# The first product of two squared-relu layers by seven half-size products

## Chip, core and metric

The kernel runs on one core of one Trainium2 chip. The metric is the device time of one execution in microseconds. The core has TensorE (PE, matrix products), VectorE (DVE), ScalarE (ACT), GpSimd (POOL) and SyncE (SP, which here issues the transfers).

## What is computed

Three transformer layers over 512 tokens of width 1024, all in float32. The first has two SwiGLU parts and a mixer, the second and third a mixer each and then a squared-relu part. The change touches the two squared-relu parts:

```python
def sq_relu_mlp(h, w1, w2):
    u = jax.nn.relu(h @ w1)
    return (u * u) @ w2
...
        x = x + sq_relu_mlp(rmsnorm_2(x, norm_mlp[layer]), w_mlp1[layer], w_mlp2[layer])
```

Here `w1` is 1024 x 4096 and `w2` is 4096 x 1024.

## The kernel before

**Layout.** Activations are held transposed, features on the 128 partitions and the 512 tokens along the row. A tile is 128 features by 512 tokens; the width 1024 is 8 tiles, the inner width 4096 is 32.

**Three matmuls for one.** To keep float32 accuracy each operand is split into a rounded part and a remainder: `hi` by an ACT copy to fp32r and `lo = x - hi` by a DVE subtract. Each product is then hi.hi + hi.lo + lo.hi, three matmuls into the same PSUM bank. Weights stream from memory in the order of `stream_plan()`, as chunks of 128 x 1024 (8 blocks of 128 x 128) that SP loads into two raw buffers `wraw`; ACT makes `whi` (L2130) and DVE `wlo` (L2435), in four buffers each (`NW = 4`). The step "split" c stands in the queues of SP, ACT and DVE. It may run when chunk c - 4 has been used by PE (`used[c - 4]`).

**The order.** `work_order()` writes out one list of steps; each engine walks this list in order and does its own part of each step, with semaphore waits between engines. `opened(key)` puts the splits of up to three chunks ahead, and `split_free` puts one when its buffer's chunk is closed, so a split stands in the queues ahead of the work on an earlier tile's result.

**A squared-relu part, `mlp(l, s, end, nxt)`.** It runs in two halves. For each of 16 feature tiles PE does 24 matmuls of 512 columns with `hhi`/`hlo` (the normalised input's parts); then the step "relu" makes the inner activation: DVE takes max(0) times the per-token scale `rb` from PSUM (L2541), ACT squares (L2173) and copies to `mhi` (L2176), DVE subtracts to get `mlo` (L2544). DVE's queue stands still between its two instructions until ACT is done:

```python
                    dve.scalar_tensor_tensor(tmps[:, q, :], banks[b][:, :], 0.0, rb[:, :], MAX,
                                             MUL).then_inc(*relu.up((s, f)))
                    w.wait_ge(*v_hi[s, f])
```

After 16 tiles come 8 output tiles of 48 matmuls each (two chunks), added to the stream `ya` by "resid" (L2536). The first four feature tiles of a part are special: three are done side by side (`side_by_side`), between them the sums of squares for the norm are paid and the reciprocal root is worked out on DVE ("rstd"), then the fourth tile runs, PE spreads the scale (L1946), ACT copies it to `rb` (L2147), and the four "relu" steps follow.

POOL does nothing in these parts before the change. Its instructions in the other stages are adds and multiplies of 128 x 512. In the mixing stage it works beside DVE: L2919 and L2925 are rotary products and sums.

## Time and profile before

| | us |
|---|---|
| median of 3 runs (2445.96 to 2446.32) | 2446.11 |
| the profiled execution, first to last instruction (its span) | 2446.3 |
| TensorE busy | 2390.1 |
| VectorE busy | 1234.3 |
| ScalarE busy | 962.0 |
| GpSimd busy | 196.0 |

The profiled execution's span stands for its own time; it lies 0.2 us above the median of the runs. "Busy" is the time in which at least one instruction of the engine was in work. Matmuls overlap in the trace, so that the pace of PE is read from the distance between starts, not from the duration of one. The first squared-relu part lies at 1482 to 1860 us, the second at about 2075 to 2440 us.

### The profile page before, as it was taken

Reading aid. Unit: us, or ns where it says so; the run is one execution under the profiler, and the core shown is the slowest. Engines: PE = TensorE matmul, PEld = TensorE weight load, DVE = VectorE, ACT = ScalarE, POOL = GpSimd, SP = SyncE. Lnnn points to the kernel's source line nnn. Section 1 sums busy time; section 2 is a strip of 40 time slices with the busy share of each in tenths; the row PEclk is TensorE's granted clock in tenths of the full one; section 3 lists DMA queues with packets and bytes.
Section 4 is the critical chain, followed back from the end, with each engine's and each line's share of the span. In section 5 each row is a group of like instructions: output and inputs, shape, how many; then the busy total and the mean of one; then the engine's idle time right before and its main releaser. Section 6 shows DMA issues by size and latency. Waiting matters only on the chain.

```text
span 2446.3 us, 28445 instructions
## 1 busy us (share of the span) xinstructions
PE 2390.1 (98%) x11206; PEld 1912.1 (78%) x11206; DVE 1234.3 (50%) x2012; ACT 962.0 (39%) x1613; POOL 196.0 (8%) x147
## 2 busy tenths in 40 slices
PE   8999999999999999999999999999999899999998
PEld 7888888777777788888887677888887677888887
DVE  5533436788654445433336855424435775532432
ACT  4323224455432334322323554313324785431432
POOL 0100100322102000100100200000001100000000
PEclk9999999999999999999999999999999999999999
DMA  4323323211222232323323113322232012333332
GB/s 144 104 87 103 98 88 102 77 52 52 70 69 72 63 108 81 101 80 110 95 83 99 59 53 103 104 94 95 95 96 64 29 46 80 97 101 95 95 95 70
DMA packets 66805, 208.50 MB, mean 85 GB/s; under 512 B 7408, under 2 KB 15856, under 8 KB 66416
## 3 DMA queue, kind: packets, MB, share of 16 engines
q1 hardware_dynamic: 66672, 206.68, 27.1%
q8 instruction: 89, 1.46, 0.2%
q14 instruction: 44, 0.36, 0.0%
HBM read 204.55 MB, written 2.10 MB: 84 GB/s over the span
## 4 chain that ended last, share of the span: by engine, by line
PE 90%; DVE 4%; ACT 3%; issue 2%; DMA 1%; POOL 0%; POOLq 0%; SPq 0%; ACTq 0%; DVEq 0%
PE bank L1842 26%; PE bank L1846 26%; PE bank L1844 26%; PE bank L2009 2%; PE bank L1971 1%; PE bank L2016 1%; PE bank L2000 1%; PE bank L2062 1%; ACT whi L2130 1%; PE bank L1917 1%; DVE wlo L2435 1%; PE bank L1913 1%; PE bank L1915 1%; DMA wraw<-in_stream 1%; PE bank L1936 1%
## 5 line engine op out<-in xcount | busy, mean ns | idle before, releaser
L2435 DVE TENSOR_TENSOR wlo<-wraw,whi 128x1024 fp32r<-128x1024 f32 (+5 forms) x436 | 487.9, 1122 | 541.9 <-ACT whi L2130 541.1
L1842 PE MATMUL bank<-hhi,whi 128*128 128x512 f32 x1736 | 693.2, 399 | 11.4 <-ACT whi L2130 9.4
L1846 PE MATMUL bank<-hhi,wlo 128*128 128x512 f32 x1736 | 681.7, 393 | 2.1 <-DVE wlo L2435 2.1
L1844 PE MATMUL bank<-hlo,whi 128*128 128x512 f32 x1736 | 680.7, 392 | 0.4 <-DVE hlo L2442 0.4
L2130 ACT ACTIVATE whi<-wraw 128x1024 fp32r<-128x1024 f32 (+5 forms) x436 | 408.9, 940 | 493.2 <-PE bank L1846 425.0
L1842 PEld LDWEIGHTS bank<-hhi,whi 128*128 128x128 f32 x1736 | 328.1, 189 | 84.2 <-ACT whi L2130 11.4
L1846 PEld LDWEIGHTS bank<-hhi,wlo 128*128 128x128 f32 x1736 | 327.7, 189 | 74.9 <-DVE wlo L2435 5.1
L1844 PEld LDWEIGHTS bank<-hlo,whi 128*128 128x128 f32 x1736 | 328.2, 189 | 67.3 <-DVE hlo L2442 2.2
L1844 PE MATMUL bank<-mlo,whi 128*128 128x512 f32 x576 | 227.8, 395 | 0.2 <-DVE mlo L2742 0.2
L1842 PE MATMUL bank<-mhi,whi 128*128 128x512 f32 x576 | 227.8, 396 | 0.0
L1846 PE MATMUL bank<-mhi,wlo 128*128 128x512 f32 x576 | 227.7, 395 | 0.0
L1842 PEld LDWEIGHTS bank<-mhi,whi 128*128 128x128 f32 x576 | 108.1, 188 | 26.7 <-ACT mhi L2287 0.4
L1844 PEld LDWEIGHTS bank<-mlo,whi 128*128 128x128 f32 x576 | 108.1, 188 | 26.7 <-DVE mlo L2742 0.5
L1846 PEld LDWEIGHTS bank<-mhi,wlo 128*128 128x128 f32 x576 | 108.1, 188 | 26.3
L2173 ACT ACTIVATE tmps<-tmps 128x512 f32<-128x512 f32 x64 | 40.5, 632 | 175.1 <-DVE tmps L2541 175.1
L2906 POOL TENSOR_TENSOR tmps<-tmps 128x512 f32<-128x512 f32 x44 | 56.5, 1285 | 613.7 <-DVE tmps L2511 464.6
L2536 DVE TENSOR_TENSOR ya<-ya,bank 128x512 f32<-128x512 f32 x71 | 48.3, 685 | 111.5 <-PE bank L1846 111.5
L2273 ACT ACTIVATE tmps<-bank 128x512 f32<-128x512 f32 x88 | 52.6, 598 | 99.5 <-PE bank L2009 97.6
L2544 DVE TENSOR_TENSOR mlo<-tmps,mhi 128x512 fp32r<-128x512 f32 x64 | 44.4, 693 | 87.3 <-ACT mhi L2176 87.3
L2919 POOL TENSOR_TENSOR ftmps<-ftmps,rs 128x512 f32<-128x512 f32 x31 | 45.2, 1459 | 377.4 <-DVE ftmps L2611 377.2
L2541 DVE SCALAR_TENSOR_TENSOR tmps<-bank,rb 128x512 f32<-128x512 f32 x64 | 44.1, 690 | 59.9 <-PE bank L1846 55.4
L2511 DVE TENSOR_TENSOR tmps<-bank,rb 128x512 f32<-128x512 f32 x44 | 30.4, 690 | 85.7 <-PE bank L1846 85.7
(419 smaller groups left out, 3094.7 us busy)
## 6 DMA issues: line engine op xcount, KB each, us to landing
wraw<-in_stream SPq DMA_DIRECT2D x343, 512.0 KB, 3.5
wraw<-in_stream SPq DMA_DIRECT2D x32, 192.0 KB, 2.4
wraw<-in_stream SPq DMA_DIRECT2D x22, 256.0 KB, 2.6
wraw<-in_stream SPq DMA_DIRECT2D x26, 128.0 KB, 2.0
wraw<-in_stream SPq DMA_DIRECT2D x8, 320.0 KB, 2.9
xa<-in_x SPq DMA_DIRECT2D x8, 256.0 KB, 6.4
out<-ya SPq DMA_DIRECT2D x8, 256.0 KB, 2.7
m<-in_mask SPq DMA_DIRECT2D x1, 1024.0 KB, 4.8
```

The lines of the kernel that those rows point to most:

```text
L1842: pe.matmul(out, sh, xh, start=first, stop=False)
L1844: pe.matmul(out, sh, xl, start=False, stop=False)
L1846: p = pe.matmul(out, sl, xh, start=False, stop=end and last)
L2009: p = pe.transpose(banks[tb][:, i * 128:i * 128 + 128], src[:, at0:at0 + 128], ident[:, :])
L2130: act.activation(whi[j][:, 0:L], wraw[i][:, 0:L], F.Copy).then_inc(*hi.up(c))
L2273: act.activation(et_of(stage, et)[:, c * 128:(c + m) * 128], banks[tb][:, 0:m * 128], F.Copy).then_inc(*turned.up((stage, u, c)))
L2435: dve.tensor_tensor(wlo[j][:, 0:L], wraw[i][:, 0:L], whi[j][:, 0:L].bitcast(f32), SUB).then_inc(*lo.up(c))
L2536: dve.tensor_tensor(ya[:, n, :], ya[:, n, :], banks[b][:, :], ADD).then_inc(*x_dve.up((nxt, n)))
L2541: dve.scalar_tensor_tensor(tmps[:, q, :], banks[b][:, :], 0.0, rb[:, :], MAX, MUL).then_inc(*relu.up((s, f)))
L2544: dve.tensor_tensor(ahl[s][1][:, f % 16, :], tmps[:, q, :], ahl[s][0][:, f % 16, :].bitcast(f32), SUB).then_inc(*v_lo.up((s, f)))
L2906: pool.tensor_tensor(tmps[:, q, :], tmps[:, q, :], tmps[:, u, :], MUL).then_inc(*gated.up((s, f)))
L2919: pool.tensor_tensor(s, s, rs[rows, :], MUL).then_inc(*rope_sin.up(key))
```

## The change

**Products.** Of each part's 32 feature tiles the first four are done as before. The other 28 go in seven blocks of four tiles. A block is a 2 x 2 product: weights 512 inputs by 256 features, activations 512 inputs by 256 tokens. In place of eight such products, `seven(f)` does seven (`q1, q7, p5, p6, q2, q4, q3`), each 24 matmuls of 256 columns into one bank; three of them go on top of an earlier one's bank. A fifth to eighth operand are sums: four of the seven weight chunks are sums that POOL makes in place in the raw buffer (`plus`, with `settled` naming the chunk whose `lo` must be made first), and four token operands are differences or sums of quarters of the input, made once for each part.

**Token operands.** POOL writes the gained input into `xa` (eight "plain" of 128 x 512), then four "token_sum" of 128 x 1024; ACT and DVE split them into `thi`/`tlo` ("token_parts"). They stand in the list behind the three side-by-side tiles, "token_parts" behind the first four "relu".

**Combining.** "first_copy" (ACT) saves q1's bank, "shared" (DVE, two instructions) builds the two common terms V and W in `ftmps`, and four "corner" steps give the quarters of the result: DVE adds or subtracts (not for `c11`), takes max and scale, ACT squares and copies, DVE subtracts.

**Stages.** A part now runs in four quarters of 8 feature tiles (two blocks; in the first quarter the four plain tiles and one block), each followed by 8 output tiles of 24 matmuls; the inner buffer holds 8 tiles in place of 16. The first two output tiles do their first four inputs ahead (`begun`), then the rest. The part has four more raw buffers, six in all.

```diff
+PRODUCTS = (("q1", 0, None, None), ("q7", 0, 1, "q1"), ("p5", 1, 2, None), ("p6", 0, 2, "q7"), ("q2", 3, None, None),
+            ("q4", 2, None, None), ("q3", 0, 3, "p6"))
+NARROW, WIDE = 2, 6
...
+    def seven(tag, blk, s, quarters):
+        at = len(raws)
+        for pair in quarters:
+            raws.append(Raw(pair, s))
+        index = {}
+        for name, raw, plus, settled in PRODUCTS:
+            index[name] = len(plan)
+            plan.append(Chunk((tag, blk, name), at + raw, 8, 128, None if plus is None else at + plus,
+                              None if settled is None else index[settled]))
+        for raw, name in ((0, "q3"), (1, "p5"), (2, "q4"), (3, "q3")):
+            raws[at + raw].gone = index[name]
...
     def mlp(l):
-        for half in range(2):
-            for f in range(16):
-                col(f"m{l}u{half}", f"mlp1_{l}", half * 16 + f)
+        s, mat = 4 + 2 * l, f"mlp1_{l}"
+        for part in range(4):
+            for b in range(2):
+                f = 8 * part + 4 * b
+                if f == 0:
+                    for n in range(4):
+                        col(f"m{l}u", mat, n)
+                else:
+                    seven(f"m{l}s", f, s, rows_and_cols([mat] * 4, (f + 2, f + 3, f, f + 1)))
             for n in range(8):
-                col(f"m{l}d{half}", f"mlp2_{l}", n, 16, half * 16)
+                add((f"m{l}d{part}", n, 0), f"mlp2_{l}", part * 8, 8, n * 128, 128, s)
...
     def mlp(l, s, end, nxt):
-        afree = (end, *x_at[7])
+        guard = afree = (end, *x_at[7])
+        put("wide", s, guard)
...
+        def seven(f):
...
+            bank, last = {}, {}
+            over = {"q2": "q1", "q4": "q7", "q3": "p5"}
+            for name, *_ in PRODUCTS:
+                c = opened((f"m{l}s", f, name))
+                if name in over:
+                    b, was = bank[over[name]], (last[over[name]],)
+                else:
+                    b = G.take()
+                    was = b.was
+                bank[name] = b
+                put("seven", s, name, c, b.i, was, name not in over)
+                closed.add(c)
+                done = ("used", c)
+                key = (s, f)
+                if name == "q1":
+                    put("first_copy", key, b.i, V.i, (done, *V.free))
+                    last["q1"] = ("first_copy", key)
+                elif name == "p6":
+                    put("shared", key, b.i, bank["q7"].i, V.i, W.i, (done, *W.free))
+                    b.free = (("combined", ("v", key)),)
+                    last["q7"] = ("combined", ("w", key))
+                    q = T.take()
+                    put("corner", key, "c22", bank["p5"].i, W.i, q.i, ("combined", ("w", key)), q.was, afree)
+                    last["p5"] = W.free = ("combined", (key, "c22"))
+                    W.free = (W.free,)
+                    q.free = (("v_lo", (key, "c22")),)
+                elif name in over:
+                    part = {"q2": "c11", "q4": "c21", "q3": "c12"}[name]
+                    q = T.take()
+                    put("corner", key, part, b.i, V.i, q.i, done, q.was, afree)
+                    q.free = (("v_lo", (key, part)),)
+                    b.free = (("relu" if part == "c11" else "combined", (key, part)),)
+                    if name == "q3":
+                        V.free = (("combined", (key, part)),)
+            return ("used", c)
...
+        for part in range(4):
+            if part == 0:
+                ts = side_by_side(("h", s), *[(f"m{l}u", n, 0) for n in range(3)])
+                paid = open_sums[R.next].tok
+                for j in range(8):
+                    put("plain", s, j, (*x_at[j], *paid))
+                    if j == 3:
+                        put("token_sum", s, 1, ())
+                for n in (3, 2, 4):
+                    put("token_sum", s, n, ())
+                ts.append(run(feat([(f"m{l}u", 3, 0)], ("h", s))))
                 R.step()
...
-                square(t, half * 16 + f)
-                f += 1
-            h_end = t.end
-            x = ("v", s, half * 16)
-            if half == 0:
+                for n in (3, 1, 2, 4):
+                    put("token_parts", s, n, guard)
+                h_end = seven(4)
+            else:
+                seven(8 * part)
+                h_end = seven(8 * part + 4)
+            x = ("v", s, 8 * part)
+            begun = [feat([(f"m{l}d{part}", n, 0)], x) for n in range(2)]
+            for tile in begun:
+                next(tile)
+            if part < 3:
                 for n in range(8):
...
+                    t = run(begun[n] if n < 2 else feat([(f"m{l}d{part}", n, 0)], x))
+                    put("resid", ("mlp", s, part), n, t.bank, (t.end, *x_at[n]))
+                    t.freed(("x_dve", (("mlp", s, part), n)))
...
-                return residual(nxt, x, lambda n: [(f"m{l}d1", n, k0) for k0, _ in groups(16)], (h_end,))
+                return residual(nxt, x, lambda n: [(f"m{l}d3", n, 0)], (h_end,), begun=begun)
...
-                ahl[s] = [sb(f"mhi{l}", [128, 16, S], f32r, ph), sb(f"mlo{l}", [128, 16, S], f32r, ph)]
+                ahl[s] = [sb(f"mhi{l}", [128, 8, S], f32r, ph), sb(f"mlo{l}", [128, 8, S], f32r, ph)]
+                tok[s] = [sb(f"thi{l}", [128, 4, 4, 256], f32r, ph), sb(f"tlo{l}", [128, 4, 4, 256], f32r, ph)]
+                wide_raw[s] = [sb(f"wraw{l}_{i}", [128, 1024], where=ph) for i in range(WIDE - NARROW)]
...
+        def quarter_of(s, name, k):
+            if name in ("q1", "q2", "q3"):
+                j = k if name == "q1" else 4 + k
+                p = slice(256, 512) if name == "q3" else slice(0, 256)
+                return hhi[:, j, p], hlo[:, j, p], h_hi[s, j], h_lo[s, j]
+            n = {"p5": 1, "p6": 2, "q7": 3, "q4": 4}[name]
+            return tok[s][0][:, n - 1, k, :], tok[s][1][:, n - 1, k, :], p_hi["token", s, n], p_lo["token", s, n]
...
+        def token_sums(n):
+            k0, k1, first, second = slice(0, 4), slice(4, 8), slice(0, 256), slice(256, 512)
+            b11, b12, b21, b22 = xa[:, k0, first], xa[:, k0, second], xa[:, k1, first], xa[:, k1, second]
+            return {1: (b11, b11, b12, SUB), 3: (b12, b12, b22, SUB), 2: (b22, b22, b11, ADD), 4: (b21, b21, b22, SUB)}[n]
...
+            f0, p = f % 8 + (2 if part in ("c11", "c12") else 0), slice(0, 256) if part in ("c11", "c21") else slice(256, 512)
+            return ahl[s][0][:, f0:f0 + 2, p], ahl[s][1][:, f0:f0 + 2, p], p
         def es_of(stage, i):
...
+            def fetch(r):
+                raw, L = raws[r], raws[r].size()
+                src = t["stream"][offs[r]:offs[r] + 128 * L].rearrange("(p l) -> p l", p=128)
+                if raw.after >= 0:
+                    w.wait_ge(*lo[raw.after])
+                if raw.fresh:
+                    for e in unlocked[raw.wide]:
+                        w.wait_ge(*at(e))
+                sp.dma_start(raw_at(r)[:, 0:L], src).then_inc(s_raw[raw.slot], 16)
+            def fetch_on(r):
+                while r < len(raws) and raws[r].after <= split and (raws[r].slot < NARROW or raws[r].wide in unlocked):
+                    fetch(r)
+                    r += 1
+                return r
...
+                elif k == "seven":
+                    s, name, c, b, was, fresh = a
+                    _, _, i = chunk(c)
+                    w.wait_ge(*hi[c])
+                    waits(was)
+                    for n in range(8):
+                        xh, xl, ev_h, ev_l = quarter_of(s, name, n % 4)
+                        out = banks[b][:, 256 * (n // 4):256 * (n // 4) + 256]
+                        sh, sl = whi[i][:, n * 128:n * 128 + 128], wlo[i][:, n * 128:n * 128 + 128]
+                        w.wait_ge(*ev_h)
+                        pe.matmul(out, sh, xh, start=fresh and n == 0, stop=False, skip_group_check=True)
+                        w.wait_ge(*ev_l)
+                        pe.matmul(out, sh, xl, start=False, stop=False, skip_group_check=True)
+                        w.wait_ge(*lo[c])
+                        p = pe.matmul(out, sl, xh, start=False, stop=n == 7, skip_group_check=True)
+                    p.then_inc(*used.up(c))
                 elif k == "mm_first":
                     tiles, cs = a
                     xh, xl, ev_h, ev_l = operand_of(tiles[0].x, 0)
...
+                        w.wait_ge(*landed(plan[c].raw))
+                    else:
+                        w.wait_ge(*pool_sum["weights", c])
                     if c >= NW:
                         w.wait_ge(*used[c - NW])
-                    act.activation(whi[j][:, 0:L], wraw[i][:, 0:L], F.Copy).then_inc(*hi.up(c))
...
+                elif k == "token_parts":
+                    s, n, guard = a
+                    dst, src, *_ = (tok[s][0][:, n - 1, :, :], token_sums(n)[0])
+                    waits(guard)
+                    w.wait_ge(*pool_sum["token", s, n])
+                    act.activation(dst, src, F.Copy).then_inc(*p_hi.up(("token", s, n)))
+                elif k == "first_copy":
+                    key, b, v, after = a
+                    waits(after)
+                    act.activation(ftmps[:, v, :], banks[b][:, :], F.Copy).then_inc(*first_copy.up(key))
+                elif k == "corner":
+                    (s, f), part, b, v, q, after, was, afree = a
+                    key = ((s, f), part)
+                    w.wait_ge(*relu[key])
+                    act.activation(tmps[:, q, :], tmps[:, q, :], F.Square).then_inc(*relu_sq.up(key))
+                    w.wait_ge(*relu_sq[key])
+                    waits(afree)
+                    act.activation(corner_of(s, f, part)[0], two(tmps[:, q, :]), F.Copy).then_inc(*v_hi.up(key))
                 elif k == "init":
                     w.wait_ge(ld["cols"], 16)
...
                                       SUB).then_inc(*lo.up(c))
+                elif k == "token_parts":
+                    s, n, guard = a
+                    w.wait_ge(*p_hi["token", s, n])
+                    dve.tensor_tensor(tok[s][1][:, n - 1, :, :], token_sums(n)[0], tok[s][0][:, n - 1, :, :].bitcast(f32),
+                                      SUB).then_inc(*p_lo.up(("token", s, n)))
+                elif k == "shared":
+                    key, b6, b7, v, u, after = a
+                    w.wait_ge(*first_copy[key])
+                    waits(after)
+                    dve.tensor_tensor(ftmps[:, v, :], banks[b6][:, :], ftmps[:, v, :], SUB).then_inc(*combined.up(("v", key)))
+                    w.wait_ge(*combined["v", key])
+                    dve.tensor_tensor(ftmps[:, u, :], banks[b7][:, :], ftmps[:, v, :], ADD).then_inc(*combined.up(("w", key)))
+                elif k == "corner":
+                    (s, f), part, b, v, q, after, was, afree = a
+                    key = ((s, f), part)
+                    vhi, vlo, p = corner_of(s, f, part)
+                    scale = rb[:, p].rearrange("q (a b) -> q a b", a=1).to_broadcast([128, 2, 256])
+                    tq = tmps[:, q, :]
+                    w.wait_ge(*rbm["h", s])
+                    w.wait_ge(*at(after))
+                    waits(was)
+                    if part == "c11":
+                        dve.scalar_tensor_tensor(two(tq), two(banks[b][:, :]), 0.0, scale, MAX, MUL).then_inc(*relu.up(key))
+                    else:
+                        if part == "c22":
+                            p = dve.tensor_tensor(tq, ftmps[:, v, :], banks[b][:, :], SUB)
+                        elif part == "c21":
+                            p = dve.tensor_tensor(tq, ftmps[:, v, :], banks[b][:, :], ADD)
+                        else:
+                            p = dve.tensor_tensor(tq, banks[b][:, :], ftmps[:, v, :], SUB)
+                        p.then_inc(*combined.up(key))
+                        w.wait_ge(*combined[key])
+                        dve.scalar_tensor_tensor(two(tq), two(tq), 0.0, scale, MAX, MUL).then_inc(*relu.up(key))
+                    w.wait_ge(*v_hi[key])
+                    dve.tensor_tensor(vlo, two(tq), vhi.bitcast(f32), SUB).then_inc(*v_lo.up(key))
                 elif k == "operand":
                     s, j, after, part = a
                     if part in (2, 3):
...
+                elif k == "split":
+                    c, = a
+                    ch = plan[c]
+                    if ch.plus is None:
+                        continue
+                    dst, src = raw_at(ch.raw), raw_at(ch.plus)
+                    w.wait_ge(*landed(ch.raw))
+                    w.wait_ge(*landed(ch.plus))
+                    if ch.settled is not None:
+                        w.wait_ge(*lo[ch.settled])
+                    w.wait_ge(*before.now())
+                    pool.tensor_tensor(dst[:, :], dst[:, :], src[:, :], ADD).then_inc(*pool_sum.up(("weights", c)))
+                    before = pool_sum
+                elif k == "plain":
+                    s, j, after = a
+                    waits(after)
+                    w.wait_ge(*before.now())
+                    pool.tensor_scalar(xa[:, j, :], X(s)[:, j, :], gain(s, j), None, MUL).then_inc(*pool_sum.up(("plain", s, j)))
+                    before = pool_sum
+                elif k == "token_sum":
+                    s, n, _ = a
+                    dst, x0, x1, op = token_sums(n)
+                    w.wait_ge(*before.now())
+                    pool.tensor_tensor(dst, x0, x1, op).then_inc(*pool_sum.up(("token", s, n)))
+                    before = pool_sum
                 elif k == "gate":
```

## Rows read from the trace of the kernel before

**Rows 1.** The page's first line: busy us (share of the span) of each engine, instructions.
```profile
PE 2390.1 (98%) x11206; PEld 1912.1 (78%) x11206; DVE 1234.3 (50%) x2012; ACT 962.0 (39%) x1613; POOL 196.0 (8%) x147
```

**Rows 2.** Waits of TensorE, 1482 to 1860 us (first squared-relu layer): us, times, longest.
```profile
PE bank L1846 <- DVE wlo L2435: 0.5, 1, 0.5
```

**Rows 3.** Timeline of TensorE, first product: start us, duration us, engine, line, operation.
```profile
1500.04 0.39 PE L1842 MATMUL bank<-hhi,whi 128*128 128x512 f32 x1
1500.27 0.39 PE L1844 MATMUL bank<-hlo,whi 128*128 128x512 f32 x1
```

**Rows 4.** Timeline of TensorE, second product.
```profile
1620.05 0.39 PE L1842 MATMUL bank<-mhi,whi 128*128 128x512 f32 x1
1620.28 0.40 PE L1844 MATMUL bank<-mlo,whi 128*128 128x512 f32 x1
```

**Rows 5.** Timeline of TensorE, the only 256-column matmuls.
```profile
668.06 0.28 PE L1913 MATMUL bank<-whi,hhi 128*128 128x256 f32 x1
668.18 0.28 PE L1915 MATMUL bank<-wlo,hhi 128*128 128x256 f32 x1
```

**Rows 6.** Timeline of VectorE, one feature tile of the first product; idle before in brackets.
```profile
1564.41 0.69 DVE L2541 SCALAR_TENSOR_TENSOR tmps<-bank,rb 128x512 f32<-128x512 f32 x1 [1.21 <-PE bank L1846]
1566.46 0.69 DVE L2544 TENSOR_TENSOR mlo<-tmps,mhi 128x512 fp32r<-128x512 f32 x1 [1.36 <-ACT mhi L2176]
1567.41 1.23 DVE L2435 TENSOR_TENSOR wlo<-wraw,whi 128x1024 fp32r<-128x1024 f32 x1 [0.26 <-ACT whi L2130]
```

**Rows 7.** Timeline of ScalarE, the same tile.
```profile
1565.13 0.63 ACT L2173 ACTIVATE tmps<-tmps 128x512 f32<-128x512 f32 x1 [3.19 <-DVE tmps L2541]
1565.80 0.63 ACT L2176 ACTIVATE mhi<-tmps 128x512 fp32r<-128x512 f32 x1
1566.34 1.05 ACT L2130 ACTIVATE whi<-wraw 128x1024 fp32r<-128x1024 f32 x1
```

**Rows 8.** The page's groups: PSUM and SBUF operand on VectorE; a PSUM copy on ScalarE.
```profile
L2536 DVE TENSOR_TENSOR ya<-ya,bank 128x512 f32<-128x512 f32 x71 | 48.3, 685 | 111.5 <-PE bank L1846 111.5
L2273 ACT ACTIVATE tmps<-bank 128x512 f32<-128x512 f32 x88 | 52.6, 598 | 99.5 <-PE bank L2009 97.6
```

**Rows 9.** Groups by form, GpSimd: count, busy us, mean ns.
```profile
L2906 POOL TENSOR_TENSOR tmps<-tmps 128x512 f32<-128x512 f32 x44 | 56.5, 1285 | 613.7 <-DVE tmps L2511 464.6 <-ACT tmps L2160 149.1
...
L2961 POOL MEMSET up<- 128x544 f32 x1 | 0.6, 551 | 84.8 <-DVE ya L2503 84.8
```

**Rows 10.** Timeline of VectorE, mixing stage.
```profile
467.52 2.32 DVE L2435 TENSOR_TENSOR wlo<-wraw,whi 128x1024 fp32r<-128x1024 f32 x1
469.77 1.21 DVE L2628 TENSOR_REDUCE sm<-bank 128x2 f32<-128x1024 f32 x1
```

**Rows 11.** Timeline of GpSimd, the same microseconds.
```profile
467.13 1.63 POOL L2925 TENSOR_TENSOR qk<-ftmps 128x512 f32<-128x512 f32 x1
```

**Rows 12.** Timeline of ScalarE, start of the first squared-relu layer.
```profile
1500.64 1.06 ACT L2130 ACTIVATE whi<-wraw 128x1024 fp32r<-128x1024 f32 x1 [3.63 <-DMA wraw<-in_stream]
1504.53 0.60 ACT L2147 ACTIVATE rb<-bank 128x512 f32<-128x512 f32 x1 [2.83 <-PE bank L1946]
```

**Rows 13.** Timeline of VectorE, the same start.
```profile
1495.68 2.58 DVE L2435 TENSOR_TENSOR wlo<-wraw,whi 128x1024 fp32r<-128x1024 f32 x2 [3.77 <-ACT whi L2130]
...
1505.16 0.69 DVE L2541 SCALAR_TENSOR_TENSOR tmps<-bank,rb 128x512 f32<-128x512 f32 x1 [2.20 <-ACT rb L2147]
...
1507.82 0.69 DVE L2541 SCALAR_TENSOR_TENSOR tmps<-bank,rb 128x512 f32<-128x512 f32 x1
```

**Rows 14.** Timeline of TensorE, the same start.
```profile
1503.44 1.05 PE L1946 MATMUL bank<-ident,rcs 128*128 128x128 f32 x8
1504.25 0.48 PE L1842 MATMUL bank<-hhi,whi 128*128 128x512 f32 x1
```

**Rows 15.** Windows: busy us of each engine, granted clock (PEclk), DMA share.
```profile
2078.00:2083.00 5.00, 4.47 (x13) 3.50 (x13) 4.16 (x6) 2.19 (x3) 0.00 (x0) 0.66 0.31 105
```

**Rows 16.** Timeline of TensorE in that window, ahead of the slow stretch.
```profile
2078.57 0.50 PE L1846 MATMUL bank<-hhi,wlo 128*128 128x512 f32 x1 [0.53 <-DVE wlo L2435]
```

More of the change, by code:

```diff
@@ L117, in stream_plan @@
     add(("uv", 0, 0), "ukv_v", 0, 1, 0, 512)
-    plan += odd_order()
+    for item in odd_order():
+        add(*item)
     for n in range(8):
@@ L147, in head_chunks @@
 def head_chunks(plan):
-    return {key: c for c, (key, *_) in enumerate(plan)}
+    return {chunk.key: c for c, chunk in enumerate(plan)}
 class Slot:
```

129 lines of the change are left out of this document (80 added, 49 removed).

## The prediction

> **What bounds the kernel now.** I read the page's busy times first: PE has work in 98% of the span [rows 1]. The waits of PE in the first squared-relu part come next: one, of 0.5 us, in 378 us [rows 2]. So here the pace of the matmuls sets the end, and the timeline gives it: 0.227 us from start to start of 512-column matmuls on the first product [rows 3], 0.233 on the second [rows 4]. A feature tile of 24 takes 5.44 us, an output tile's 24 take 5.6. DVE and ACT have room, but only as a sum. On their timelines one tile is a chain: DVE 0.69, then 1.36 of waiting while ACT squares and copies, DVE 0.69, then 0.26 of waiting for ACT's `whi`, then `wlo` 1.23 [rows 6, 7]. That is 4.2 us of 5.44. The change lengthens this chain and shortens PE's side, so the two must be laid beside each other product by product.
>
> **PE's side.** The only 256-column matmuls start 0.120 us apart [rows 5]. A block before: 96 x 0.2267 = 21.76 us. After: 168 x 0.120 = 20.16 us, 2.88 for a product. The gain is 1.60 us a block, not an eighth of 21.76 (2.72), since half the columns cost more than half the time. Operands in the inner buffer's region run 3% slower [rows 3, 4]; if the token sums do, 0.3 us of it is lost. Fourteen blocks: 22.4 us at most, if nothing else binds.
>
> **DVE and ACT in one block.** Seven splits: 7 x 1.23 = 8.6 us on DVE. V and W (2), three corners with combine (3 each), `c11` (2): 13 instructions of about 0.69 [rows 6, 8], 9.0 us. Each corner holds DVE for 1.36 us more while ACT works: 5.4. Together 23.0 us, more than PE's 20.2 and than the 21.8 before, though DVE is busy for only 17.6 of it. The saved bank copy (0.60) [rows 8] is ACT's and fits.
>
> **POOL beside DVE.** A weight sum of 128 x 1024 isn't in the trace; twice the 128 x 512 row [rows 9] is 2.5 us, four to a block. What it does to DVE the mixing stage shows: a `wlo` that takes 1.23 us alone takes 2.32 when it starts at 467.52 in a POOL instruction that ends at 468.76; 468.76 + 1.08 is its end [rows 10, 11]. So it stood until POOL was through. The reduction from PSUM behind it keeps its 1.21. I take it that a DVE instruction with two SBUF operands and a POOL add take turns: `wlo`, `mlo` and the scale of a combined corner wait, those with a PSUM operand don't. Bounds: no waiting, and 2.5 us for each of four adds.
>
> The Trainium skill, "SBUF — State Buffer", "Who interferes with whom", speaks against this change in the same sense: a two-SBUF-input VectorE instruction and a GpSimd one that reads SBUF exclude each other, and whichever comes second stands for the other's whole length. By that rule the sum below stays; without it it is the second rival's.
>
> **A pair of blocks A, B and two output tiles** (three pairs to a part), in us from PE's start of A. The splits of q1, q7, p5 are done ahead in the output stage before. PE runs A at its pace to 20.2. DVE cannot begin V before p6 is done (11.7, with the 0.2 us that DVE starts after PE's end in [rows 6]): V, W, `c22` to 16.6; `wlo` of B's q1 18.1; POOL adds for q7 to 20.7, so `c11` ends at 21.4; POOL adds for p5 to 23.9, so `wlo` of q7 ends 25.1; POOL adds for p6 to 27.65, so `c21` ends 30.4; `wlo` of p5 31.9; `c12` 35.3; `wlo` of p6 36.8; POOL adds for q3 to 39.3; `wlo` of q2, q4, q3: 40.6, 41.8, 43.0; V and W 44.3. PE needs `wlo` for each product's third matmul (2.64 us remain) and W for q4: q7 ends 27.8, p5 34.6, p6 39.5, q2 43.2, q4 47.2, q3 50.1 (at its own pace 40.3). DVE goes on: `c22` 47.8, a split 49.3, `c11` 52.0, a split 53.4, `c21` 56.8, a split 58.3, `c12` 61.8. The two output tiles' first halves are A's features: done at 55.8. Their second halves want `c21` (56.1 for `hi`), then `c12` (61.0): the first tile ends 62.9, the second 65.8. Before, 8 x 5.44 + 11.2 = 54.7. Each pair costs 11.1 us; six cost 66.6. The remaining six output tiles have 5.6 us for some 3 us of DVE and give a full start to the next pair.
>
> **The first quarter.** Queues, in the order of the list: q7's split stands behind the first side-by-side tile; then POOL gets eight "plain" and four token sums; then comes p5's split, whose sum is behind all of these on POOL; and on ACT that split stands ahead of `rb`, of the four squares and of "token_parts" (today it is the split at 1500.64, with `rb` behind it [rows 12]). q7 on PE needs the first "token_parts". So: `wlo` of q1 at 1496.9 [rows 13], q7's sum 1499.4, eight "plain". Their price isn't in the trace: between the memset of 544 that reads nothing, 0.55, and the two-input 1.28 [rows 9]; I take 0.9 as the middle, 7.2. Token sums 4 x 2.5, p5's sum 2.5, and 3.0 for DVE's turns (one `wlo` and some nine small root instructions): 1522.1. From there: POOL's sum for p6 blocks `wlo` of p5 (2.5 + 1.2), four corners at 2.66 apart [rows 13] with the last one's end (10.7), then token `hi` and `lo`, less overlap 1.5: q7 can go at 1538.0. PE, done with q1 soon after the root, stands about 25 us. Six products from there, V and W waiting for three `wlo` and a sum of POOL, end 18.1 later, `c12` 29.7 later, two output tiles 33.7 later: 1571.7. Before: 1504.25 [rows 14] + 4 x 5.44 + 11.2 = 1537.2. Loss 34.5 us, twice 69.
>
> The Trainium skill, "GPSIMD Engine Reference", "Engine selection", calls one-input instructions roughly line-rate; by the memset row "plain" would then be 0.55, and both parts together 5.6 us cheaper.
>
> **Clock.** At 2078 us PE waited 0.53 us more after a string of short waits, and its granted clock was then at the lower level, 1.2 of 2.4 GHz: 0.66 as the mean of 5 us [rows 15, 16]. Some ten matmuls took twice their 0.227: 2 us. I take one such fall for each pair and each first quarter, eight in all: 16 us (bounds: 0, and three in each, 48).
>
> **What costs nothing.** The eight more "resid" for each quarter (0.69 us in 5.6) lie under PE's tile. SP loads four 512 KB pieces for a block, as many bytes as before for four tiles, into six buffers; the earliest bound on a fetch is `lo` of a chunk long done. In the first quarter new raw buffers wait for the stage before to end, but then POOL doesn't want them for 10 us. If that cover failed, a fetch is late by some 3 us once a part. Inner buffers of 8 tiles are written again from 11 us after their last reader.
>
> **Sum.** 2446.3 + 66.6 + 69.0 + 16.0 = 2597.9, less the 0.2 us by which the profiled execution lies above the median: 2597.7.
>
> **Rivals.**
> 1. *PE stays the bound* (other side). DVE and ACT would have to fit 23.0 us of chain into 20.2, the token operands be there in time. Then 2446.1 - 22.4 = 2423.7. It decides if a corner's wait of 1.36 falls under 0.6 us and q7's token parts are ready by 1507; both speak against it in the queues. Chance 0.03.
> 2. *POOL and DVE don't hinder one another.* The pair's chain is then: `c12` of A 31.2, PE ends B at 44.7, output tiles 60.3, a loss of 5.6; the first quarter loses 28.5. 2446.1 + 33.6 + 57 + 16 = 2552.7. Against it, the row of 2.32 us. Chance 0.20.
> 3. *Only the first quarter's stand counts*; the pairs are absorbed: 2446.1 + 69 - 12 x 1.6 = 2496. For it: only two blocks follow one another. Chance 0.06.
> 4. *Starved PE stays at the low clock for longer*, three falls at each place: 2597.7 + 32 = 2630, with dearer POOL sums up to 2650. Chance 0.14.
> 5. *As I forecast*, 2575 to 2620: 0.52. The other 0.05 are small changes near 2446.
>
> **Range.** 2545 to 2640 holds cases 2, 5 and most of 4. What this kernel's measurement tells from no change is about 0.2%, 5 us. Faster 0.04, same 0.02, slower 0.94.
>
> **What would show it.** PE's waits in both parts: one of 20 to 30 us on token parts at about 1510 (and none if I misread the queue); two of about 3 us for each pair, on `hi` or `lo` of B's p5 and p6, and one on ACT's inner copy in the first output tile. DVE: 1.36 us ahead of each corner's last subtract. `wlo` of 2 to 3.7 us beside POOL (all at 1.23 would mean rival 2). Matmul starts 0.120 apart in a product. I'd be wrong if POOL's 1024-wide sum isn't near 2.5, if "token_parts" doesn't stand behind p5's split, or if blocks gain more slack from the output stage than four chunks.

## The result, and the profile after

The changed kernel takes 2594.8 us (median of 4 runs, 2593.4 to 2596.4) against 2446.0 us, a ratio of 1.061 (95% interval 1.060 to 1.063). The forecast was 2597.7, slower. The profiled execution took 2596.35 us, its span is 2594.5. The page's first line answers to [rows 1]: TensorE has work for 93% of the span, where it was 98%, and all other engines are busier.

```profile
PE 2411.8 (93%) x12214; PEld 1963.3 (76%) x12214; DVE 1407.3 (54%) x2164; ACT 1019.9 (39%) x1677; POOL 378.9 (15%) x227
```

Most of the lost time stands in PE's waits of the first squared-relu layer, which were one of 0.5 us before [rows 2]. From 1482 to 2000 us (line waited for; us in total, times, longest; the row left out belongs to the stage behind the layer):

```profile
PE bank L2026 <- ACT thi L2321: 31.8, 1, 31.8
PE bank L2008 <- ACT mhi L2333: 10.7, 4, 2.7
PE bank L2030 <- DVE wlo L2638: 8.1, 10, 1.7
PE bank L2026 <- ACT whi L2315: 7.3, 3, 2.5
...
PE bank L2026 <- DVE ftmps L2651: 2.4, 3, 0.8
```

One wait of 31.8 us for the first `thi`, a piece of the token sums; and several in each pair of blocks, all for ScalarE's or VectorE's output. The timeline of PE gives the lengths of the stages. First quarters, from the first product of the layer to the first product of the second quarter, take 137.7 us (1477.2 to 1614.9) and 134.7 in the second layer. Each later quarter, a pair of blocks and eight output tiles, takes 99.4 to 100.9 us, mean 100.1. For the same stretches without any block I use the staging-only kernel below (`f0_quarters_alone`): 97.0 and 94.8, and 88.36. So the first quarters lose 40.7 + 40.0 = 80.7 us and the six pairs, 600.5 us together against 6 x 88.36 = 530.2, lose 70.3; 151.0 in all. The two spans differ by 148.2: the stretches outside the two layers, whose code the change leaves as it was, take 2.8 us less. They scatter by more than that from run to run: the first layer starts anywhere from 1472.6 to 1477.2 us in the ten profiled kernels.

**One pair.** TensorE starts it at 1614.94, runs half-size products 0.12 us apart as foreseen from [rows 5], and starts the next pair at 1714.29:

```profile
1614.94 0.29 PE L2026 MATMUL bank<-hhi,whi 128*128 128x256 f32 x1
...
1616.75 0.28 PE L2026 MATMUL bank<-hhi,whi 128*128 128x256 f32 x1
1616.87 0.28 PE L2028 MATMUL bank<-hlo,whi 128*128 128x256 f32 x1
...
1714.29 0.28 PE L2026 MATMUL bank<-hhi,whi 128*128 128x256 f32 x1
```

VectorE in the middle of it (start, duration, operation; idle before in brackets):

```profile
1626.58 0.69 DVE L2649 TENSOR_TENSOR ftmps<-bank,ftmps 128x512 f32<-128x512 f32 x1 [0.52 <-PE bank L2030]
...
1630.81 0.69 DVE L2674 TENSOR_TENSOR mlo<-tmps,mhi 128x512 fp32r<-128x512 f32 x1 [1.36 <-ACT mhi L2333]
1631.76 1.23 DVE L2638 TENSOR_TENSOR wlo<-wraw,whi 128x1024 fp32r<-128x1024 f32 x1 [0.26 <-ACT whi L2315]
1632.90 0.68 DVE L2662 SCALAR_TENSOR_TENSOR tmps<-bank,rb 128x512 f32<-128x512 f32 x1
1634.95 1.22 DVE L2674 TENSOR_TENSOR mlo<-tmps,mhi 128x512 fp32r<-128x512 f32 x1 [1.36 <-ACT mhi L2333]
1636.74 2.77 DVE L2638 TENSOR_TENSOR wlo<-wraw,whi 128x1024 fp32r<-128x1024 f32 x1 [0.58 <-ACT whi L2315]
...
1640.14 2.39 DVE L2672 SCALAR_TENSOR_TENSOR tmps<-tmps,rb 128x512 f32<-128x512 f32 x1
```

and POOL's adds in the same microseconds:

```profile
1633.21 2.40 POOL L3150 TENSOR_TENSOR wraw<-wraw 128x1024 f32<-128x1024 f32 x1 [13.15 <-DVE wlo L2638]
1635.76 2.67 POOL L3150 TENSOR_TENSOR wraw<-wraw,wraw 128x1024 f32<-128x1024 f32 x1
1639.59 2.39 POOL L3150 TENSOR_TENSOR wraw<-wraw,wraw 128x1024 f32<-128x1024 f32 x1 [1.16 <-DVE wlo L2638]
```

Read the two lists together. The 1.36 us of idle time ahead of each corner's last subtract are the same as in [rows 6]. The subtract at 1634.95 takes 1.22 instead of 0.69, and the sum of POOL beside it ends at 1635.61. The `wlo` at 1636.74 takes 2.77 instead of 1.23, with POOL's second sum ending at 1638.43. The scale at 1640.14 takes 2.39 instead of 0.69, with POOL's third ending at 1641.98. Each ends 0.55 to 1.1 us after POOL's, a little less than it takes alone (0.69 and 1.23). The stand goes both ways: POOL's second sum starts while that subtract is in work and takes 2.67 in place of 2.40. The instructions with a PSUM operand (1632.90) keep their 0.68.

**The first quarter.** The queue of POOL, with the new "plain" instruction on L3156:

```profile
1501.20 2.40 POOL L3150 TENSOR_TENSOR wraw<-wraw,wraw 128x1024 f32<-128x1024 f32 x1 [87.83 <-DVE wlo L2638]
1503.81 1.57 POOL L3156 TENSOR_SCALAR xa<-ya,cols 128x512 f32<-128x512 f32 x1 [0.21 <-POOL wraw L3150]
1505.55 1.83 POOL L3156 TENSOR_SCALAR xa<-ya,cols 128x512 f32<-128x512 f32 x1 [0.17 <-POOL xa L3156]
...
1520.34 7.17 POOL L3162 TENSOR_TENSOR xa<-xa 128x1024 f32<-128x1024 f32 x3
1527.65 4.83 POOL L3150 TENSOR_TENSOR wraw<-wraw,wraw 128x1024 f32<-128x1024 f32 x2
```

and ScalarE, where the split at 1530.02 stands in front of `rb` and the squares, as its counterpart at 1500.64 did in [rows 12], but now waits 25.33 us for POOL:

```profile
1530.02 1.06 ACT L2315 ACTIVATE whi<-wraw 128x1024 fp32r<-128x1024 f32 x1 [25.33 <-POOL wraw L3150]
1530.98 0.58 ACT L2350 ACTIVATE rb<-bank 128x512 f32<-128x512 f32 x1
...
1543.33 3.89 ACT L2321 ACTIVATE thi<-xa 128x1024 fp32r<-128x1024 f32 x4
```

TensorE then goes on, with 0.21 us from start to start in place of 0.12:

```profile
1544.52 0.55 PE L2026 MATMUL bank<-thi,whi 128*128 128x256 f32 x1 [31.77 <-ACT thi L2321]
1545.68 0.58 PE L2028 MATMUL bank<-tlo,whi 128*128 128x256 f32 x1 [0.61 <-DVE tlo L2643]
1546.06 0.41 PE L2030 MATMUL bank<-thi,wlo 128*128 128x256 f32 x1
1546.28 0.41 PE L2026 MATMUL bank<-thi,whi 128*128 128x256 f32 x1
```

### The profile page after: what moved, and what is told of

It is laid out like the page before. It is cut to its first block, busy times and chain, and to the rows that moved or that the text cites. A ratio compares the mean times of both kernels' runs of the same rounds, so it can differ in the third digit from the quotient of the medians.

```text
span 2594.5 us, 30999 instructions
## 1 busy us (share of the span) xinstructions
PE 2411.8 (93%) x12214; PEld 1963.3 (76%) x12214; DVE 1407.3 (54%) x2164; ACT 1019.9 (39%) x1677; POOL 378.9 (15%) x227
## 4 chain that ended last, share of the span: by engine, by line
PE 75%; DVE 9%; ACT 7%; issue 6%; POOL 3%; DMA 1%; POOLq 0%; SPq 0%; DVEq 0%; ACTq 0%
PE bank L2008 20%; PE bank L2010 20%; PE bank L2012 20%; ACT whi L2315 3%; PE bank L2191 2%; DVE tmps L2672 2%; DVE wlo L2638 1%; ACT tmps L2330 1%; PE bank L2028 1%; PE bank L2030 1%; PE bank L2026 1%; PE bank L2153 1%; PE bank L2198 1%; POOL xa L3156 1%; POOL wraw L3150 1%
## 5 line engine op out<-in xcount | busy, mean ns | idle before, releaser
L2638 DVE TENSOR_TENSOR wlo<-wraw,whi 128x1024 fp32r<-128x1024 f32 (+3 forms) x478 | 570.1, 1199 | 520.8 <-ACT whi L2315 520.2
L2315 ACT ACTIVATE whi<-wraw 128x1024 fp32r<-128x1024 f32 (+3 forms) x478 | 452.4, 950 | 595.4 <-PE bank L2012 436.5
L2008 PE MATMUL bank<-hhi,whi 128*128 128x512 f32 x1288 | 518.0, 402 | 12.3 <-ACT whi L2315 10.4
L2012 PE MATMUL bank<-hhi,wlo 128*128 128x512 f32 x1288 | 506.3, 393 | 1.6 <-DVE wlo L2638 1.6
L2010 PE MATMUL bank<-hlo,whi 128*128 128x512 f32 x1288 | 505.4, 392 | 0.4 <-DVE hlo L2680 0.4
L2008 PE MATMUL bank<-mhi,whi 128*128 128x512 f32 x576 | 235.0, 408 | 21.8 <-ACT mhi L2333 21.4
L3150 POOL TENSOR_TENSOR wraw<-wraw,wraw 128x1024 f32<-128x1024 f32 x50 | 123.1, 2462 | 633.4 <-DVE wlo L2638 631.1
L2026 PE MATMUL bank<-thi,whi 128*128 128x256 f32 x448 | 134.1, 299 | 83.8 <-ACT thi L2321 63.5
L2026 PEld LDWEIGHTS bank<-thi,whi 128*128 128x128 f32 x448 | 91.8, 205 | 86.6 <-issue 69.7
L2030 PE MATMUL bank<-thi,wlo 128*128 128x256 f32 x448 | 134.3, 300 | 14.7 <-DVE wlo L2638 14.7
L2028 PE MATMUL bank<-tlo,whi 128*128 128x256 f32 x448 | 132.3, 295 | 1.2 <-DVE tlo L2643 1.2
L2330 ACT ACTIVATE tmps<-tmps 128x512 f32<-128x512 f32 x56 | 35.3, 631 | 186.9 <-DVE tmps L2672 160.4
```

The source lines that it names most:

```text
L2008: pe.matmul(out, sh, xh, start=first, stop=False)
L2010: pe.matmul(out, sh, xl, start=False, stop=False)
L2012: p = pe.matmul(out, sl, xh, start=False, stop=end and last)
L2026: pe.matmul(out, sh, xh, start=fresh and n == 0, stop=False, skip_group_check=True)
L2028: pe.matmul(out, sh, xl, start=False, stop=False, skip_group_check=True)
L2030: p = pe.matmul(out, sl, xh, start=False, stop=n == 7, skip_group_check=True)
```

## The experiments

The theory has three parts: a pair is paced by VectorE's chain through the corners; POOL's sums stretch that chain because the two engines take turns; the first quarter loses to a queue. The main rivals are that the turns cost nothing (the forecast's second) and that waiting for the sums' *result*, not their company, is what costs. Each ratio below is to the kernel before as it ran beside the experiment: 2443.5 us for the first four, 2445.65 for the other four.

**Without the sums.** The output isn't the reference's: blocks whose weights should be sums use the first of the two raw blocks.

```diff
-                    if plan[c].plus is None:
-                        w.wait_ge(*landed(plan[c].raw))
-                    else:
-                        w.wait_ge(*pool_sum["weights", c])
+                    w.wait_ge(*landed(plan[c].raw))
...
-                    pool.tensor_tensor(dst[:, :], dst[:, :], src[:, :], ADD).then_inc(*pool_sum.up(("weights", c)))
...
+                    continue
```

> The changed kernel without GpSimd's weight sums: the seven products take the raw weight blocks unsummed, so the first product of both squared-relu layers isn't the reference's. Nothing else moves. My theory (token operands late in the first quarter, and in the pairs a chain of DVE and ACT that POOL lengthens by about 7 us through the shared read interface and through its own 2.4 us): a pair with its eight output tiles falls from 100.0 to about 92.2 us, and in the first quarter p5's split no longer stands behind the token work on POOL, so that TensorE's wait of 31.8 us for the token parts ends some 28 us sooner; total about 2478 us. If POOL and DVE did not hinder one another and only the corners' round trips counted, a pair would stay at 98 us or more. If all the loss were POOL's, a pair would come to 88.4 or less, as before the change.

Measured: 2513.98 us, ratio 1.029 (1.027 to 1.030). The pairs take 93.3 to 94.5, mean 94.1, and the first quarters 112.3 and 110.7. A pair lies between the two conditions (98 or more, 88.4 or less): POOL's sums are a part of its loss, not the whole. The total lies 36 us above my estimate: a pair fell by 6.0 in place of 7.8 and a first quarter by 25.4 and 24.0 in place of 28, and these terms of mine add up to 2492, not to 2478.

**The same sums, with nobody waiting for their result.** POOL adds a tile of the same size that no one reads, at the same places but for the first block. The output again isn't the reference's, for the same reason.

```diff
-                    dst, src = raw_at(ch.raw), raw_at(ch.plus)
+                    if ch.key[1] == 4:
+                        continue
...
+                    spare = xa[:, 0:2, :]
...
-                    pool.tensor_tensor(dst[:, :], dst[:, :], src[:, :], ADD).then_inc(*pool_sum.up(("weights", c)))
+                    pool.tensor_tensor(spare, spare, spare, ADD).then_inc(*pool_sum.up(("weights", c)))
```

> As the run without weight sums, but GpSimd makes in the six pairs an add of the same size at the same place of its queue on spare memory, for which nobody waits (none in the first block of a layer). So the sums' own time is off everybody's path and only their presence beside VectorE is left. If a GpSimd add and a VectorE instruction with two SBUF operands exclude one another, a pair stays near 99.5 us (100.0 with real sums) and the total is about 2522 us. If they don't, it equals the run without sums, a pair at 92 and about 2478 us in total.

Measured: 2536.11 us, 1.038 (1.036 to 1.039), pairs of 97.8 to 98.9, mean 98.5. The total is 14 us above my estimate, but what decides is the pair: 98.5 against 94.1 without sums. So some 4.4 of a pair's 11.7 us come from the company alone. A spare sum takes 1.89 us and a real one 2.40, so that the real sums' company should cost more; no run shows that by itself. The windows of one pair in the kernel without sums, in this one and in the changed kernel show it in VectorE's busy time, the third figure behind the length: 49.55, 53.72 and 56.34 us for the same 56 instructions.

```profile
1587.30:1681.80 94.50, 89.33 (x530) 78.69 (x529) 49.55 (x56) 33.20 (x40) 0.00 (x0) 0.96 0.28 90
```
```profile
1588.10:1685.90 97.80, 91.11 (x530) 79.68 (x528) 53.72 (x56) 33.19 (x40) 15.41 (x8) 0.95 0.27 87
```
```profile
1614.90:1714.30 99.40, 90.21 (x530) 78.28 (x529) 56.34 (x56) 33.41 (x40) 19.46 (x8) 0.97 0.26 85
```

On VectorE's timeline of the kernel with spare sums, a scale stands from 1612.28 until just past the end of a spare sum that runs from 1611.73 to 1613.62. Nothing connects the two by data:

```profile
1612.28 1.89 DVE L2669 SCALAR_TENSOR_TENSOR tmps<-tmps,rb 128x512 f32<-128x512 f32 x1
```
```profile
1611.73 1.89 POOL L3151 TENSOR_TENSOR xa<-xa 128x1024 f32<-128x1024 f32 x1 [1.16 <-DVE wlo L2635]
```

**The queue of the first quarter.** The fourth side-by-side tile is put in the list ahead of the plain tiles and the token sums, and with it the split of p5, so that POOL's sum for it stands ahead of them too.

```diff
+                ts.append(run(feat([(f"m{l}u", 3, 0)], ("h", s))))
                 for j in range(8):
                     put("plain", s, j, (*x_at[j], *paid))
...
-                ts.append(run(feat([(f"m{l}u", 3, 0)], ("h", s))))
```

> The changed kernel with one thing moved: the fourth plain feature tile, and with it the split of p5, stands ahead of the eight gains and four token sums in the order. If the queue order is what makes the first quarter late, p5's weight sum runs at about 1504 to 1506 us, the four squares follow at once, and the token parts wait only for GpSimd's 14 us of gains and two sums: TensorE's wait falls from 31.8 to about 14 us in each layer, total about 2557 us. The pairs stay at 100 us. If the token sums' own time were the whole reason, the wait would stay above 25 us and the total above 2580.

Measured: 2572.91 us, 1.053 (1.051 to 1.054). The token wait falls from 31.8 to 12.7 us, the first quarters shorten by 13.2 and 11.5, and pairs stay near 100. That the queue order is the cause of most of the stand is shown. The wait itself came out near the 14 us that I expected; the total missed by 16 us, because the quarter doesn't keep all of the 19.1 us. In the first layer some 3 us come back ahead of the wait (the root is done later, and `q1` runs in part at the lower clock) and 2.9 behind it, where `tlo` takes 10.16 us in place of 4.63 beside POOL's sums. POOL's three token sums take 8.07 instead of 7.17 us with VectorE active beside them:

```profile
1525.12 10.16 DVE L2643 TENSOR_TENSOR tlo<-xa,thi 128x1024 fp32r<-128x1024 f32 x4 [4.97 <-ACT thi L2321]
```
```profile
1521.65 8.07 POOL L3162 TENSOR_TENSOR xa<-xa 128x1024 f32<-128x1024 f32 x3
1529.87 3.19 POOL L3150 TENSOR_TENSOR wraw<-wraw,wraw 128x1024 f32<-128x1024 f32 x1
```

**The chain through the corners.** A corner is cut into two entries of the list, and a weight split goes between them, where VectorE would stand for 1.36 us. The work is the same.

```diff
+                    split_free()
+                    put("corner_act", key, "c22", q.i, afree)
+                    put("corner_lo", key, "c22", q.i)
...
-                elif k == "corner":
-                    (s, f), part, b, v, q, after, was, afree = a
+                elif k == "corner_act":
+                    (s, f), part, q, afree = a
...
+                elif k == "corner_lo":
+                    (s, f), part, q = a
```

> The changed kernel with the next weight split put inside the corner (for c22, c21 and c12): ACT makes the next chunk's high part ahead of square and copy, and VectorE its low part while ACT works on the corner, so that the 1.36 us of standing is used. If the corner's round trip in VectorE's in-order queue is a main part of the pair's chain, a pair falls from 100.0 to about 91.5 us and the total to about 2535. If VectorE against GpSimd at the read interface is the only bound in a pair, a pair stays at 98 or more and the total above 2580.

Measured: 2528.08 us, 1.034 (1.033 to 1.036), pairs of 90.2. The split now fills the gap, and the last subtract waits 0.23 us:

```profile
1619.63 1.22 DVE L2645 TENSOR_TENSOR wlo<-wraw,whi 128x1024 fp32r<-128x1024 f32 x1
1621.08 0.69 DVE L2685 TENSOR_TENSOR mlo<-tmps,mhi 128x512 fp32r<-128x512 f32 x1 [0.23 <-ACT mhi L2340]
```

The order alone gives back 9.9 of the 11.7 us. Its sums of POOL are as before (20.05 us in the pair), and the granted clock doesn't fall in it (1.00, the sixth figure behind the length):

```profile
1605.20:1695.40 90.20, 86.16 (x529) 75.97 (x528) 55.38 (x56) 33.67 (x40) 20.05 (x8) 1.00 0.29 94
```

The first quarters, 132.6 and 130.5, shorten by 5.1 and 4.2; their wait of 31.8 us is unchanged, as it has another cause.

**Both cures.** The edits of the kernel without sums and of this one together (the output isn't the reference's, as there).

> Both cures together: the split inside the corner, and no weight sums (so the first products of both squared-relu layers aren't the reference's). If the pair's excess of 11.7 us over 88.4 is made of VectorE's standing in the corners, the read interface and the wait for the sums, and of nothing else, a pair comes near TensorE's own pace, 14 x 2.88 + 44.9 = 85.2 us, allowing 1 to 2 us at the seam to the output tiles: 85 to 87.5; total about 2467 us. If something else binds (the 256-column pace, the banks, the transfers), a pair stays at 89 or more.

Measured: 2451.21 us, 1.0024 (1.0015 to 1.0033), pairs of 85.1 to 85.2. PE has work in 84.91 of 85.10 us of this pair, at the full clock:

```profile
1585.00:1670.10 85.10, 84.91 (x529) 75.78 (x528) 48.90 (x56) 33.45 (x40) 0.00 (x0) 1.00 0.32 99
```

So with both cures a pair gains on the staging alone: 88.4 - 85.2 = 3.2 us. The total is 16 us below my estimate of 2467, the pair within its range. It isn't below the kernel before, because the first quarters still take 108.8 and 106.3 us against 97.0 and 94.8, which eats the six gains of 3.2.

**The staging alone.** The changed kernel with all first products as plain tiles: quarters, inner buffer of 8 tiles and six raw buffers stay.

```diff
-                    seven(f"m{l}s", f, s, rows_and_cols([mat] * 4, (f + 2, f + 3, f, f + 1)))
+            for n in range(8 * part, 8 * part + 8):
+                add((f"m{l}u", n, 0), mat, 0, 8, n * 128, 128, s if n > 3 else None)
...
-                h_end = seven(4)
...
+            for f in range(8 * part + (0 if part else 4), 8 * part + 8):
+                t = run(feat([(f"m{l}u", f, 0)], ("h", s)))
+                square(t, f)
+            h_end = t.end
```

> The staging alone: inner buffer of 8 tiles, four quarters, output tiles of 24 matmuls with the first two begun ahead, six raw buffers; no half-size products and no token sums, all 32 feature tiles as before. By my sum this costs nothing: within 3 us of the kernel before, a quarter of 8 tiles with its output tiles at 88.4 us. If the staging were a part of the loss, a quarter would take 90 or more.

Measured: 2444.7 us, 1.0000 (0.9991 to 1.0009). The smaller pieces, the additional "resid" and the buffers cost nothing that can be measured.

**One block at a time.** The first quarter is all plain tiles; each later quarter is one block, then four plain tiles, so six blocks instead of fourteen. The token sums are made on POOL beside the first quarter's tiles and split among its output tiles. The output is the reference's.

```diff
+            if part:
+                f = 8 * part
+                seven(f"m{l}s", f, s, rows_and_cols([mat] * 4, (f + 2, f + 3, f, f + 1)))
+            for n in range(8 * part + (4 if part else 0), 8 * part + 8):
+                add((f"m{l}u", n, 0), mat, 0, 8, n * 128, 128, s if n > 3 else None)
...
+                    if part == 0 and n in (1, 2, 3, 4):
+                        put("token_parts", s, (None, 3, 1, 2, 4)[n], guard)
```

> Quarters of one block and then four plain tiles (first quarter all plain, with the token sums on GpSimd beside it and their parts made between its output tiles): six blocks of seven products in place of fourteen, each followed by 21.8 us in which VectorE can catch up. If the chain of VectorE and ACT with its 30 us for a block is the bound only because blocks follow one another or the output tiles at once, TensorE's pace holds: 6 x 1.6 = 9.6 us less than before, ratio about 0.996. If a single block loses already, the ratio is 1.000 or above.

Measured: 2434.87 us, 0.9955 (0.9941 to 0.9968), 11 us less than the kernel before: a small gain, but clear of the noise; foreseen were 9.6. PE has no wait that the trace lists from 1574 to 1834 us, and a quarter takes 86.5:

```profile
1574.10:1660.60 86.50, 86.50 (x457) 73.96 (x456) 43.47 (x48) 29.89 (x36) 9.60 (x4) 1.00 0.30 98
```

The corners' chain, with its 1.36 us of standing, now lies under the four plain tiles that follow the block. POOL's sums hardly meet it: in this quarter three of the four run in the output stage, from 1646.65, and only two `wlo` are longer than 1.23 us (1.54 and 1.88). So this kernel takes away both causes of a pair's loss at once and doesn't part them.

**The same with the split between the corners' halves.** The last kernel with the edit of the chain experiment.

> As the run with one block in a quarter, with the next split inside the corner as well. If there the chain is hidden anyway, it equals that run within 0.1%; if not, it is up to 3 us faster. Ratio to the kernel before about 0.996.

Measured: 2436.16 us, 0.9960 (0.9948 to 0.9973). Nothing is gained: what is under cover needs no cure.

## Why the prediction was right, and where its terms were off

**A block on PE.** Foreseen 20.16 us at 0.120 us a matmul; the one-block kernel's block takes 19.95, since matmuls on the token sums start 0.118 apart (the forecast allowed only for their being slower). A quarter with one block takes 86.54 us against 88.36, a gain of 1.8, not 1.60. The pair with both cures gains only 3.2 for two blocks, as its output tiles take 0.5 us longer.

**The pair.** The step-by-step timeline held. V began 11.6 us after A's start (at 1626.58), `c22`'s last subtract ended at 16.6, `c11`'s at 21.2 and A's `c12` at 34.5 (foreseen 11.7, 16.6, 21.4 and 35.3), the stretched instructions stand where the forecast had them, and a pair lost 11.7 us against 11.1. Of the waits that were to show it, the one on B's p5 (2.5 us) and the one on ACT's inner copy (2.7) came; a second of 3 us on p6 did not, but four on `wlo` of at most 1.4. The runs divide the loss: 5.7 are VectorE's chain without any sum (94.1 against 88.4; falls of the clock come with it), 4.4 are the company of the shorter spare sums (98.5), and 1.6 (100.1) are the real sums' greater length and the wait for their result, which no run parts. The edit of the chain alone takes away more than its share: 9.9 with the sums and 8.9 without them (94.1 to 85.2). So the parts don't simply add. With the sums VectorE's busy time falls by only 1.0 us of it (56.34 to 55.38); that the clock no longer falls is another part (below), and the rest no run divides.

**Turns between POOL and VectorE.** The term was read from a single row of 2.32 us [rows 10], and it is now shown by the spare sums, which nobody waits for. The Trainium skill, "SBUF — State Buffer", "Who interferes with whom", has the same rule, and this trace agrees in length too: a scale of 0.69 that starts at 1640.14 beside a sum takes 2.39 us, to 0.55 after the sum's end. A sum took 2.40 us, against the 2.5 put in.

**The first quarter.** The stand came from the queue that I named, but it was undersized: 34.5 foreseen, 40.7 and 40.0 measured. The forecast had p5's sum end at 1522.1; it ended at 1530.0. Of these 7.9 us 3.2 lie ahead of the layer, whose first product starts at 1477.20 against 1473.98, and are no part of the 40.7; 4.7 are the layer's. Four terms make most of them. The first `wlo` came another 0.8 us later within the layer (1499.74 against 1495.68 in [rows 13], less the 3.2). "Plain" was priced at 0.9 as a middle between 0.55 and 1.28 [rows 9], but takes 1.56 and 0.17 of gap: 8 x 0.83 = 6.6 us more. VectorE's turns took some 0.5 us from POOL, not the 3.0 put in. The four token sums were 0.5 shorter (2.38 + 7.17 against 10). That is 0.8 + 6.6 - 2.5 - 0.5 = 4.4. From p5's sum on, q7's first matmul comes after 14.5 us and its second, which needs `tlo`, after 15.7; 15.9 were foreseen. From there to the end of the second output tile it takes 35.7 us against 33.7; the first product, q7, runs at the lower clock there, 0.21 us a matmul. So 4.7 - 0.2 + 2.0 = 6.5 account for the 6.2 by which the first layer's quarter lost more than foreseen (40.7 - 34.5). The term of the forecast that was off is thus the price of an instruction that the trace didn't have: it lay outside both bounds.

**Clock.** Sixteen us were put down for eight falls. The falls come, and fifteen of them are new: two in each first quarter (one is the long stand) and eleven in the six pairs. (One more in each layer, in the side-by-side tiles, is there before the change too.) Of the first pair's 99.4 us, these three and these four are near half the full clock:

```profile
1648.00:1651.00 3.00, 2.72 (x14) 2.43 (x13) 1.92 (x2) 2.97 (x6) 0.00 (x0) 0.56 0.33 132
1674.00:1678.00 4.00, 3.18 (x7) 2.26 (x8) 1.92 (x2) 1.68 (x3) 0.00 (x0) 0.57 0.23 94
```

The first fall of a pair should cost little, since PE waits for VectorE's `wlo` again behind it (at 1650.97 here); I read that from the order of the waits, and no run shows it by itself. The second is paid in full. It follows the wait for ACT's inner copy, and from there to the end of the pair PE has no wait above 0.2 us:

```profile
1674.82 0.79 PE L2008 MATMUL bank<-mhi,whi 128*128 128x512 f32 x1 [2.71 <-ACT mhi L2333]
...
1676.56 0.63 PE L2008 MATMUL bank<-mhi,whi 128*128 128x512 f32 x1
1676.99 0.63 PE L2010 MATMUL bank<-mlo,whi 128*128 128x512 f32 x1
```

The starts are 0.43 us apart in place of 0.234. From 1674.82 to the end of the pair the matmuls take 1.6 us more than 0.234 each, over the six pairs 1.6 to 3.1, mean 2.2; in the kernel with the split between the halves, where the clock doesn't fall, the same stretch has 0.5. So about 1.7 us of a pair's loss are the clock's, an estimate from these rows, 10 in six pairs against 12 foreseen, and most of the difference between the first two pairs (99.4 and 100.9) is this (1.6 and 2.8). That leaves 10.0 for the chain, against 11.1. For the totals, 69 + 4 were foreseen for the first quarters and 80.7 measured, 66.6 + 12 and 70.3 for the pairs: 7.7 too little and 8.3 too much. That the total was within 3 us is luck to that extent: two errors of opposite sign, and 2.8 us outside the layers.

**Rivals.** The first (PE stays the bound) describes the pairs with both cures and the quarters with one block, not the changed kernel. The second (no turns) is excluded by the spare sums. The third (only the first quarter) is excluded by the pairs' 11.7. The fourth wanted three falls at each place, 24; there are fifteen, and a pair's cost some 1.7 us, not 6.

## What to carry to other kernels

Fewer operations on the engine that sets the pace are worth only what the others can follow: lay their chains, with the waits between engines, beside the new stretch product by product, and interleave the new work with old work before stacking it. Six blocks, each followed by four plain tiles, and a first quarter without one turned a loss of 6% into a gain of 0.45%. A wait of TensorE can cost more than its length: behind 2.7 us of waiting stood another 1.7 of slower matmuls. An instruction of another engine's queue that waits for a late sum holds all that stands behind it; look at the order of the list first. Price a new instruction by a row with the same operands, or keep both bounds wide.

## What the runs showed of the hardware that was not expected

POOL's `TENSOR_SCALAR` of 128 x 512 with one scalar for each partition takes 1.56 us, more than the two-tensor add of that size, 1.285 [rows 9]. The Trainium skill, "GPSIMD Engine Reference", "Engine selection", calls one-input instructions roughly line-rate; this measurement doesn't show it. An add of 128 x 1024 whose two inputs are the same tensor takes 1.89 us, with two tensors 2.40.

Small instructions of VectorE are held up beside POOL too, by an amount that depends on what POOL has in work. In the changed kernel the eleven of the root's chain from 1505.87 run beside "plain": nine take 0.15 or 0.16, and two 0.47 and 0.54.

```profile
1506.06 0.47 DVE L2614 TENSOR_SCALAR rcs<-sm 128x4 int32<-128x4 int32 x1
1506.56 0.16 DVE L2617 TENSOR_TENSOR newt<-rcs 128x4 f32<-128x4 f32 x1
...
1507.74 0.54 DVE L2617 TENSOR_TENSOR newt<-rcs 128x4 f32<-128x4 f32 x1
```

In the kernel without weight sums the same chain meets a token sum, and one of the eleven stands to the sum's end, 2.33 us in place of 0.16; in the one-block kernel one takes 2.20.

```profile
1501.04 2.33 DVE L2618 SCALAR_TENSOR_TENSOR rcs<-newt,rcs 128x4 f32<-128x4 f32 x1
```
```profile
1500.96 2.40 POOL L3152 TENSOR_TENSOR xa<-xa 128x1024 f32<-128x1024 f32 x1
```

The granted clock is at the lower of its two levels (1.2 of 2.4 GHz) while PE stands in the first quarter, and still when PE has work again, up to about 1552; then the full clock is back. Windows of that time:

```profile
1518.00:1544.00 26.00, 0.00 (x0) 0.00 (x0) 7.47 (x9) 7.15 (x11) 13.78 (x7) 0.50 0.06 20
1544.00:1552.00 8.00, 6.87 (x32) 6.61 (x33) 7.05 (x7) 6.53 (x8) 1.70 (x1) 0.52 0.01 2
1552.00:1560.00 8.00, 8.00 (x70) 8.00 (x69) 6.48 (x6) 1.21 (x3) 1.56 (x1) 1.00 0.46 153
```
